# A decoder layer on eight cores: the first weight panels of the merge requested at the beginning of the attention's last quarter

## The reference

```
o      = diff_attention(q, k, v)                  # 8 heads, two softmax maps each, causal
o      = rms_norm(o) * (1 - lambda) * silu(z_attn)
y_attn = o @ w_o_attn                             # 1024 -> 2048
u      = layer_norm(conv31(glu(glu_in)))
u      = silu(u) * silu(z_conv)
y_conv = u @ w_pw2 + b                            # 1024 -> 2048
m      = sigmoid(gate_attn) * y_attn + sigmoid(gate_conv) * y_conv
x      = x + rms_norm(m @ w_out)                  # 2048 -> 2048
```

## Time and profile before

| what | us |
|---|---|
| median of 3 runs (1170.3 to 1328.04) | 1173.33 |
| the profiled execution | 1171.47 |
| its span on the slowest core (core 3) | 1169.9 |
| spans of the eight cores | 1162.9 to 1169.9 |
| TensorE busy, of the span | 1092.9 (93%) |
| VectorE busy | 520.5 (44%) |
| ScalarE busy | 397.2 (34%) |
| GpSimd busy | 119.0 (10%) |

### The profile page before, as it was taken

How to read it: one execution, slowest core, us unless ns; L and a number is a source line. 1 busy time by engine, 2 the same in 40 slices (tenths; PEclk the granted TensorE clock), 3 DMA queues, 4 the chain that set the end, 5 groups by cost and what they waited for, 6 DMA issues and landing times.

```text
span 1169.9 us, 22516 instructions; the slowest of 8 cores (1162.9 to 1169.9 us)
## 1 busy us (share of the span) xinstructions
PE 1092.9 (93%) x8326; PEld 664.6 (57%) x8326; DVE 520.5 (44%) x1180; ACT 397.2 (34%) x567; POOL 119.0 (10%) x212
## 2 busy tenths in 40 slices
PE   0798999889999999999999999879999999999997
PEld 0466667655655587766766765435555555554443
DVE  3573566567754112355364364514333333331444
ACT  3342445543111016666666666511111111110211
POOL 0211111111000000011010001301101111000000
PEclk9899999999999999999999999879999999999999
DMA  6969787859543342032020000394368754637443
GB/s 149 210 160 176 163 178 165 179 129 188 120 93 76 76 96 37 28 63 46 19 64 27 2 27 2 38 180 66 56 96 144 137 91 85 121 73 173 151 145 143
DMA packets 56085, 121.98 MB, mean 104 GB/s; under 512 B 6048, under 2 KB 21664, under 8 KB 52896
## 3 DMA queue, kind: packets, MB, share of 16 engines
q0 software_dynamic: 27648, 62.93, 32.8%
q1 hardware_dynamic: 27744, 56.81, 16.0%
q10 hardware_dynamic: 576, 0.70, 0.2%
HBM read 168.05 MB, written 15.27 MB: 157 GB/s over the span
## 4 chain that ended last, share of the span: by engine, by line
PE 84%; DMA 5%; issue 3%; DVE 3%; ACT 3%; SPq 0%; POOL 0%; DVEq 0%; ACTq 0%; POOLq 0%
PE ps L1352 16%; PE ps L823 14%; PE ps L777 11%; PE ps L1417 8%; PE ps L942 7%; PE ps L656 7%; PE ps L911 5%; PE ps L1076 4%; PE ps L1367 4%; PE ps L1356 4%; DMA r<-usc 2%; PE ps L700 2%; DMA hTx<-wop 2%; DMA r<-xf 1%; DMA usc<-uT 1%
## 5 line engine op out<-in xcount | busy, mean ns | idle before, releaser
L918 ACT ACTIVATE r<-ps 128x1024 bf16<-128x1024 f32 (+2 forms) x192 | 185.9, 980 | 109.8 <-PE ps L911 106.1
L1352 PE MATMUL ps<-hTo,wring 128*128 128x448 bf16 x1024 | 205.5, 360 | 5.6 <-DMA wring<-wp 5.6
L164 POOL DMA_DIRECT2D wring<-wp x176 | 93.6, 550 | 701.9 <-PE ps L1352 196.4
L1352 PEld LDWEIGHTS ps<-hTo,wring 128*128 128x128 bf16 x1024 | 101.3, 99 | 104.7 <-issue 14.2
L942 PE MATMUL ps<-r 128*128 128x129 bf16 x1456 | 118.2, 220 | 6.0 <-DVE r L991 1.5
L656 PE MATMUL ps<-hTo,wring 128*128 128x320 bf16 (+1 forms) x768 | 111.4, 308 | 9.6 <-ACT hTo L552 4.0
L1374 ACT ACTIVATE zoz<-zoz 128x448 f32<-128x448 f32 x64 | 36.8, 576 | 237.8 <-DVE zoz L1373 237.8
L942 PEld LDWEIGHTS ps<-r 128*128 128x128 bf16 x1456 | 94.9, 97 | 29.0 <-issue 17.0
L777 PE MATMUL ps<-wring,hTo 128*128 128x256 bf16 x896 | 105.9, 273 | 0.3 <-PE ps L911 0.3
L656 PEld LDWEIGHTS ps<-hTo,wring 128*128 128x128 bf16 x768 | 77.4, 102 | 42.6 <-issue 13.9
L823 PE MATMUL ps<-hTo,wring 128*128 128x448 bf16 x512 | 98.3, 352 | 0.0
(11 more groups left out here) (131 smaller groups left out, 1054.3 us busy)
## 6 DMA issues: line engine op xcount, KB each, us to landing
wring<-wp POOLq DMA_DIRECT2D x176, 256.0 KB, 7.5
r<-xf SPq DMA_DIRECT2D x28, 320.0 KB, 4.3
hTx<-wop POOLq DMA_DIRECT2D x8, 1024.0 KB, 15.5
r<-usc SPq DMA_DIRECT2D x32, 231.2 KB, 8.3
hTo<-xr SPq DMA_DIRECT2D x7, 1024.0 KB, 8.4
r<-xf SPq DMA_DIRECT2D x7, 640.0 KB, 9.2
r<-ks SPq DMA_DIRECT2D x8, 512.0 KB, 4.3
r<-wout POOLq DMA_DIRECT2D x4, 1024.0 KB, 18.1
```

What stands on the lines that cost most here:

```text
L164: eng.dma_start(out=it[1][0], in_=it[1][1]).then_inc(self.dsem[it[2]], 16)
L918: t.op('act', lambda e: e.activation(out=et[:, :, 0:w], in_=src, func=AF.Exp, scale=0.125), reads=[('ps', pb), ('ps', pb + 1)], writes=[(' ...
L1352: t.op('pe', lambda e, dc=dc, k=k, w=w: e.matmul(bank(b0 + k, n), lhsT=w[:, dc, cs], rhs=hTo[:, dc, HALO + c0:HALO + c0 + n], start=(dc == ...
```

## The change

Panels 28 and 29, `wop` 0 and (on an odd core) `wop` 1 are issued at the beginning of the last quarter, ahead of its fillers; panel 30 is issued when unit 5 of `z_conv` is through (its slot held that unit's panel), panel 31 as the last filler. The five loads behind the attention loop are gone, and `f_begin` loads `wop` 1 on an even core only. The two functions move up unchanged.

```
+    def f_load(n):
+        load_panel(P_F + n, n % 4)
+
+    def wop_load(pi):
+        t.dma('pool', wopb[pi % 2].rearrange("p w a n -> p (w a n)"), io["wop"][pi], writes=[('wop', pi % 2)], key=('wop', pi % 2))
+
     att = att_stream()
...
         if g == 3:
             t.handover(oth_res + lnbuf + ['cw', ('lj', 0), ('lj', 1)], ozT_all + [('wop', 0)] + ([('wop', 1)] if NX else []))
+            f_load(0)
+            f_load(1)
+            for k in range(2 if NX else 1):
+                wop_load(k)
...
                     fill += zc_pieces(cc, k, fb)
+                    if (cc, k) == (5, NG - 1):
+                        fill.append(lambda: f_load(2))
...
         assert g < 3 or not turns
+        if g == 3:
+            fill.append(lambda: f_load(3))
...
-    f_load(0)
-    f_load(1)
-    wop_load(0)
-    f_load(2)
-    f_load(3)
...
-        wop_load(1)
+        if not NX:
+            wop_load(1)
```

More of the change, by code:

```diff
@@ L1312, in program @@
         run_first(lazy)
[L1315 to L1319, removed]
     def woutA_load(q4):
```

## The result

On the same chip the kernel after has a median of 1156.04 us (1152.08 to 1156.7, four runs), the kernel before 1171.82 us (from 1169.48 up, four runs): a ratio of 0.9856 [0.9834, 0.9879], 15.8 us less from median to median. Single executions far above the others, such as the 1328.04 us of the kernel before, are disturbed and stay out of the ratios; without that one the median before is 1170.3 us, and the difference 14.3. The forecast was 1155.9 us. The profiled execution of the kernel after took 1152.08 us, against 1171.47 before.

What follows compares the result with a forecast made beforehand. The merge stood behind loads asked for only after attention, with TensorE's clock lowered meanwhile. Slowest core 5, 1167.0 - 13.5 = 1153.5, with 0.5 for the clock 1154, plus 0.3 entries and 1.57 around the span: 1155.9 us, range 1152 to 1159.

Steps and rivals of the forecast that it cites:

- Step 1: Attention's last product to third merge piece: 21.2 us with loads early, against 39.35 on core 3, which gains 18.1.
- in parts: Core 3's gain at the merge divided: 8.4 us waits, about 7.9 heads' matmuls at lower clock, 1.85 tails.
- Rival 1: Step to the merge: only the waits go, the clock still falls; gain 8.4 us, time 1163; chance 0.07.
- Step 2: Merge tails: a clock fall behind the transposes is chance, 0 to 1.85 us; 0.5 taken as mean.
- Step 3: GpSimd's queue at the last quarter's start: moved issues at 0.54 us each cost odd cores 0, even cores 0 to 1.6.
- Step 4: Transfers of the moved loads: they land by 710, more than 40 us before use, so stay hidden.
- Step 5: Last quarter's filler list: two more entries, 0 to 0.8 us each, 0.3 taken together.
- Rival 2: Last quarter pays through late GpSimd products or rearranged fillers: 3 to 6 us on an odd core, 1159 to 1162; chance 0.11.
- Step 6: Transposes at the merge need VectorE's last two heads, done at 764.5; TensorE's heads end at 768.5, leaving 4 us.
- Rival 3: Last quarter's loads don't come forward in effect, as GpSimd reaches them late or they land late; 1171; chance 0.03.
- Rival 4: Even cores' quarter start: each DMA issue amid attention costs several times its price; at 2.47 us, time 1169; chance 0.03.

Runs made afterwards that it cites:

- fewer-matmuls run: Kernel before, with unused matmuls set in TensorE's waits at the step to the merge, 48 on an odd core and 60 on an even one; 1170.23 us, ratio 0.9981.
- run without entries: Kernel after, but panels 30 and 31 are loaded behind the attention loop, with no entries in the list of fillers; 1158.01 us, ratio 0.9871.
- split run: Kernel after, with panels 28 and 29 in 16 DMAs each instead of 4, every piece under its own name; 1161.64 us, ratio 0.990.

## Why the prediction was right, step by step

The time, 1156.04 us against 1155.9, and the way to it agree, with one division inside step 1 that was wrong. That they agree to 0.1 us is luck: the same kernel had 1158.13 in its repeat, and its profiled execution 1152.08, though the sum was made from the profiled execution before.

- **Step 1, the sum**: right. 21.2 us were worked out for the step on odd cores, 21.07 stand there, on all four; 18.9 on even ones, 18.7 (20.4 on two, where the clock fell). Core 5 gained 13.7 for 13.5, core 3 18.1 for 18.1. That core 5 would be the last was not borne out; core 7 is, by where its quarter starts.
- **Step 1, "in parts"**: wrong. It took the heads' matmuls at the lower clock, about 7.9 us, as time of their own beside 8.4 of waits, and "the granted clock says why" stood for the difference between 39.35 and 21.2. Most of them lay under the transfer. The fewer-matmuls run held the clock at 1.00 and the projection started no earlier; on core 3 the parts are 14.7 for the late load and 3.4 for the clock behind it, 1.7 of these in the tails. The sum was not touched, because it was made from the whole stretch and not from the parts.
- **Rival 1** did not come about: the clock is 1.00 through both heads. Its price of 8.4 holds for its own case, in which the matmuls stay slow with nothing left to hide them.
- **Step 2, the tails' clock as chance**: right. It fell on none of the four odd cores in the profiled execution (on two of the even ones, which have no part in the end), and on one of four in the run without entries and in the repeat, at 1.7 us each; 0 to 1.85 had been allowed.
- **Step 3, GpSimd's queue**: right on odd cores (6.56 us idle ahead of the product). On even ones the product started at 582.88 with its input ready at 580.63, 2.2 us late where 0 to 1.6 was forecast, and their quarter is shorter than before all the same. The price of 0.54 an issue was measured again as 0.53 with 31 of them in a row. The pause came with panel 28's issues, on an odd core some 50 us ahead of where the sum had it (last section).
- **Step 4, hidden transfers**: right; TensorE has no wait for a load at this step on any core.
- **Step 5, the entries**: 1.0 us on an odd core where 0.3 was taken for both, inside the bound of 0 to 0.8 each. On even cores they gave 1.8 back, which was not foreseen; it has no part in the end. Rival 2 is true to this extent, 1 us of its 3 to 6, by the entries and not by late products.
- **Step 6**: VectorE is through at 758.67 + 3.77 = 762.44 on core 3, and the second head's last matmuls start at 764.95 and take 1.5 us: the margin of 4 us is there.
- **Rival 3** falls with step 4. **Rival 4** was the right mechanism with a price that doesn't occur: the split run shows the even cores pay for each issue ahead of the product once their idle stretch is used up, and shows it at 0.53 us, not at 2.5.

The even cores' product of step 3, in GpSimd's timeline on core 0 of the kernel after, answers to the earlier trace rows:

```profile
575.69 0.60 POOL L164 DMA_DIRECT2D wring<-wp  x1
578.33 3.24 POOL L164 DMA_DIRECT2D wring<-wp  x6 [2.04 <-issue]
...
582.88 0.94 POOL L1086 TENSOR_TENSOR r<-uT,r 128x384 f32<-128x384 bf16 x1
```

## What to carry to other kernels

Where a stage opens with a load, work out its start from the bytes queued ahead of that load, not from the sum of the waits that the trace prints: slow matmuls between two waits may lie under the same transfer, and then a higher clock alone gains nothing until the load has landed. Move such a load up by its place in the queue first; here an issue 5 us ahead, but in the right order, did as well on half of the cores as one 75 us ahead. And price what the moved issues push back on the issuing engine: behind nine the product was 2.2 us late and the quarter no longer than before, behind 33 it was 14.3 us late, and the quarter grew by 11.5.

## What was not expected of the hardware

GpSimd pauses once for about 2 us in the middle of its DMA issues: 749.9 to 751.84 before, 622.10 to 624.02 on core 3 after (621.50 + 0.60 to 624.02), 576.29 to 578.33 on core 0. It looks as if it belonged to the first issue of a series, but the count settles it: in all thirteen traces, on all eight cores, a pause of 1.8 to 2.2 us stands ahead of the 114th DMA that GpSimd issues, wherever that falls. The two kernels with panels in pieces, with 216 issues instead of 192, have it once more, ahead of the 212th. Why at these two counts is open. So the change moved the pause because it moved the issues.

What makes the start of the quarter differ by several microseconds can be read from the same traces. Take the time that a core lost to the lower clock ahead of the quarter (each stretch times one minus its granted clock, 3.4 to 15.4 us) and TensorE's idle time there, from its first matmul on. Start less these two is the same for all 52 even cores of the thirteen traces, 533.8 us with a standard deviation of 0.5, where the starts themselves have 2.0; for the odd cores it is 639.7 with 1.3, against 3.0. So the scatter is mostly clock and waits; what brings them on in one execution and not in another is open. Also open is why the same two entries lengthen the quarter of one half of the cores and shorten that of the other.
